# Attention heads finished at every second unit: the head two back is transposed, then scores, then its values; compressed values as split rows in one fp32r matmul each

## The chip, the cores and the metric

The kernel runs as one program on one core of a Trainium2 chip. The metric is the device time of one execution, in microseconds (us). Three runs of the kernel before took 2580.71, 2580.88 and 2580.91 us; the median is 2580.88.

A core has a matrix engine (PE), which reads its stationary operand by a weight load (PEld) and streams the moving one; a vector engine (DVE); a scalar engine (ACT); GpSimd (POOL); and SP, whose queue issues the weight DMAs here. Each engine runs its own instructions in their written order and waits for the others by semaphores.

## The reference, cut to what matters

The program is a stack of layers on x (1, 256, 2048) in fp32: a Mamba2 mixer, a conv FFN, a sparse attention mixer (NSA), a second conv FFN. The change touches the attention alone. There are 16 heads in 4 key groups (KVG = 4, HPG = 4 heads in each), 128 values per head, 256 positions (two chunks of L = 128). With 256 positions each query sees compressed keys (15 of them), all earlier selected blocks, and the window:

```python
q = rms_norm(q.reshape(bsz, seq, G, HG, DH), q_norm)
p_c = masked_softmax(einsum('btghd,bngd->bghtn', qb, k_cmp) * scale, cmp_end <= t)
o_c = einsum('bghtn,bngd->btghd', p_c, v_cmp)          # 15 compressed keys
p_s = masked_softmax(...);  o_s = einsum(p_s, vg)      # selected blocks
p_w = masked_softmax(...);  o_w = einsum(p_w, vwb)     # window
o = gb[0] * o_c + gb[1] * o_s + gb[2] * o_w
return o @ w_out
```

## The kernel before, in words

**Every projection is streamed in units.** A unit is 8 blocks of 128x128 fp32 weights (512 KB). SP loads it into one of RING = 4 slots of `raw` (L386 on); ACT rounds it to `w_hi` (fp32r, L441); DVE forms `w_lo` = `raw` - `w_hi` (L1268); PE multiplies 8 blocks with two fp32r matmuls each, one of `w_lo` on 256 columns (L843) and one of `w_hi` on 512 (L844). ACT may round unit v + 4 only when PE has used unit v, because both share a slot:

```python
if not isinstance(w, int) or w >= RING:
    act.wait_ge(unit_used, w - RING + 1)
```

DVE's split of unit v + 4 then waits for that rounding. Two units make a tile of 128 outputs. When a tile is complete (after an odd unit), ACT copies one half of its sums (`take_cross`, L450) and DVE adds and scales it (`tile_sum`, L1273 and L1277).

**The query phase** (`q`) has four bodies of 8 units, v = 0 to 7, and each body gives the queries of the four heads of one group. Body g computes the queries of group g, while the attention of group G = g - 1 is woven between its units. The order on each engine is written out by hand in `attend`, `before` and `q_body`: what stands there for unit v is issued after PE's unit v, and on ACT and DVE before or after the round or the split of unit v + 4. Body 0 has no attention, body 1 is that of G = 0, and a loop runs bodies 2 and 3 (G = 1 and 2). Group 3 comes in `last_heads`, among the first four units of the output projection `nsa_out`.

**One head** goes through these steps, each in a function of one engine:
- `scores` (PE, L1124 to L1127): four fp32 matmuls of 143, 271, 128 and 256 columns.
- `mask` and `shift` (DVE, L1608 to L1627): mask, row maxima, and the shift `nm` for the exponentials. For a group's first head, `shift` first takes the reciprocal `rq` of the query norms (L1625), which PE has turned into columns (`turn_query_roots`, L1114).
- `exps` (ACT, L724): six exponentials with sums.
- `normalise` (DVE, L1635 to L1647): reciprocal of the sums, gates, and the scaling of the probabilities. It raises `probs_ready`.
- `turn_probs` (PE, L1137 and L1139): seven transposes of the probabilities into `pq`.
- `pt0_copy` (ACT, L730, L731) and `pt1_copy` (DVE, L1652): PSUM to SBUF.
- `outputs` (PE, L1151 and L1154): six fp32 matmuls of 128 columns on the values, two more on the 15 compressed values.
- `o_round` (ACT, L735) and `o_rest` (DVE, L1658): the head's output as high and low parts.

In the kernel before, PE does `scores(h)` and `outputs(h - 2)` after even unit 2h and `turn_probs(h - 1)` after the odd unit behind it. `query_sums` and `query_roots` form the norms of a group's queries once for each group.

Of the kernel before, what the change touches and what calls it, by code (L numbers as in the profile page):

```python
# [54 lines left out]
ROWS = 32  # L55

# [87 lines left out]
def trunk(nc, x_in, consts_in, head_in, w_ssm_in, w_ssm_out, w_gu0, w_gu1, w_down0, w_down1, w_nsa_in,  # L144
# [19 lines left out]
    with ctx:  # L164
# [58 lines left out]
        with ExitStack() as st:  # L223
# [12 lines left out]
            vcn = sb("vcn", [ROWS + NCMP, KVG, P], F32, st)  # L236
            vcs = sb("vcs", [ROWS + NCMP, P], F32, st)
# [22 lines left out]
            pts = [kv[:, 8:12].rearrange("p (b a) t -> p b (a t)", b=2), q[:, 9:13].rearrange("p (b a) t -> p b (a t)", b=2)]  # L260
            v_st = kv[:, 6:8].rearrange("p a t -> p (a t)")
# [66 lines left out]
        vcmp_moved, vcn_zero = sem("vcmp_moved"), sem("vcn_zero")  # L328
        kdiag_ready, kbc_done = sem("kdiag_ready"), sem("kbc_done")
# [98 lines left out]
        def _(act):  # L428
# [299 lines left out]
            def pt0_copy(G, h):  # L728
                act.wait_ge(turned_p, G * HPG + (h + 1))
                act.activation(pts[h % 2][:, 0, 0:3 * L], ps[6][:, 0:3 * L], ACT.Copy)  # L730
                act.activation(pts[h % 2][0:ROWS + NCMP, 0, 3 * L:4 * L], ps[6][0:ROWS + NCMP, 3 * L:4 * L], ACT.Copy).then_inc(pt0_ready, 1)  # L731

# [5 lines left out]
            def query_roots(G):  # L738

                act.wait_ge(qss_done, G + 1)  # L740
                act.wait_ge(qstd_turned, G)
                act.activation(psq[:], ps[6][:, 0:T], ACT.Sqrt, bias=eps[:, 1:2]).then_inc(qstd_ready, 1)

            def before(G, v):

                if v == 1:
                    o_round(G, 2)
                    pt0_copy(G, 3)
                if v == 3:
                    o_round(G, 3)  # L750

            def attend(G, v):

                if v == 0:
                    query_roots(G)
                if v >= 5 and v % 2:
                    o_round(G, v // 2 - 2)
                if v >= 3 and v % 2:
                    pt0_copy(G, v // 2 - 1)
                if v % 2:  # L760
                    exps(G, v // 2)

            def q_body(g):
                p = ph["q"]
                for v in range(p.body):
                    round_unit(p.unit0 + RING + v, UNIT, g, p.body)
                    if v % 2:
                        take_cross(p, g, v // 2)
                    if not is_body(g, 0):
                        if not is_body(g, 1):  # L770
                            before(g - 2, v)
                        attend(g - 1, v)
# [19 lines left out]
            def last_heads(G):  # L792

                o_round(G - 1, 2)
                query_roots(G)
# [26 lines left out]
        def _(pe):  # L822
# [276 lines left out]
            def query_sums(G):  # L1099

                pe.wait_ge(qsq_ready, HPG * (G + 1))
                if not is_body(G, 0):
                    pe.wait_ge(pt0_ready, HPG * G - 1)
                for h in range(HPG):
                    mm = pe.matmul(ps[6][h * ROWS:(h + 1) * ROWS, 0:T], ones[:, 0:ROWS], qsq[:, h], start=True, stop=True)
# [24 lines left out]
            def turn_probs(G, h):  # L1130
# [4 lines left out]
                for b in range(2):  # L1135
                    for a in range(3):
                        mm = pe.transpose(ps[6 + b][:, a * L:(a + 1) * L], prs[u][:, b, a * L:(a + 1) * L], ident[:])  # L1137
                    if b == 0:
                        pe.transpose(ps[6][0:ROWS + NCMP, 3 * L:4 * L], prc[:, u].rearrange("p c n -> p (c n)")[:, 0:ROWS + NCMP], ident[:])  # L1139
                mm.then_inc(turned_p, 1)  # L1140

            def outputs(G, h):
# [14 lines left out]
            def before(G, v):  # L1157

                if v == 0:
                    outputs(G, 2)  # L1160
                if v == 1:
                    pe.wait_ge(qstd_ready, G + 2)
                    turn_probs(G, 3)
                if v == 3:
# [12 lines left out]

            def q_body(g):
                if is_body(g, 1):
                    pe.wait_ge(k_ready, 5)  # L1180
                for v in range(ph["q"].body):
                    gemm_unit(ph["q"], g, v, xn)
                    if not is_body(g, 0):
                        if v == 1:
                            turn_query_roots(g - 1)
                        if is_body(g, 1):
                            attend(g - 1, v)
                        elif v == 0:
                            attend(g - 1, v)
                            before(g - 2, v)  # L1190
                        else:
                            before(g - 2, v)
                            attend(g - 1, v)
# [25 lines left out]
            def last_heads(G):  # L1219

                scores(G, 0)
# [37 lines left out]
        def _(dve):  # L1259
# [370 lines left out]
            def normalise(G, h):  # L1630
# [29 lines left out]
            def before(G, v):  # L1660

                if v == 0:
                    normalise(G, 3)
                if v == 1:
                    o_rest(G, 2)
                    pt1_copy(G, 3)
                if v == 3:
                    o_rest(G, 3)
# [280 lines left out]
```

## Time and profile before

| what | value |
|---|---|
| median of 3 runs | 2580.88 us |
| the profiled execution | 2582.43 us |
| its span in the profile | 2580.7 us |
| PE busy | 2571.8 us (100%) |
| DVE busy | 1791.1 us (69%) |
| ACT busy | 1424.0 us (55%) |
| POOL busy | 223.2 us (9%) |

The profiled execution took 1.73 us more than its span. The table is read from the top: PE is busy through all of the span, and the others have slack on the average. The query phase with attention lies at about 1598 to 1765 us of the span.

### The profile page before, as it was taken

Reading aid. Unit: us, or ns where it says so; the run is one execution under the profiler, and the core shown is the slowest. Engines: PE = TensorE matmul, PEld = TensorE weight load, DVE = VectorE, ACT = ScalarE, POOL = GpSimd, SP = SyncE. Lnnn points to the kernel's source line nnn. Section 1 sums busy time; section 2 is a strip of 40 time slices with the busy share of each in tenths; the row PEclk is TensorE's granted clock in tenths of the full one; section 3 lists DMA queues with packets and bytes.
Section 4 is the critical chain, followed back from the end, with each engine's and each line's share of the span. In section 5 each row is a group of like instructions: output and inputs, shape, how many; then the busy total and the mean of one; then the engine's idle time right before and its main releaser. Section 6 shows DMA issues by size and latency. Waiting matters only on the chain.

```text
span 2580.7 us, 46167 instructions
## 1 busy us (share of the span) xinstructions
PE 2571.8 (100%) x15247; PEld 2257.7 (87%) x15247; DVE 1791.1 (69%) x2590; ACT 1424.0 (55%) x2206; POOL 223.2 (9%) x199
## 2 busy tenths in 40 slices
PE   9999999999999999999999999999999999999999
PEld 8888888888888888888888888888888888888888
DVE  8777777765677777776555686777777777775444
ACT  6776766754455555554444455666555555554443
POOL 0211122222100000000111000102200000000000
PEclk9999999999999999999999999999999999999999
DMA  6665555656555556556666676334555556556665
GB/s 212 230 196 195 190 197 194 199 172 189 187 191 189 187 189 191 190 188 187 188 189 193 193 233 200 124 98 134 184 191 188 188 190 191 191 186 186 189 191 167
DMA packets 139483, 481.59 MB, mean 187 GB/s; under 512 B 17329, under 2 KB 19441, under 8 KB 138384
## 3 DMA queue, kind: packets, MB, share of 16 engines
q1 hardware_dynamic: 136448, 467.20, 57.8%
q0 software_dynamic: 2368, 12.68, 1.4%
q8 instruction: 47, 0.77, 0.1%
q10 hardware_dynamic: 592, 0.71, 0.1%
q14 instruction: 28, 0.23, 0.0%
HBM read 478.28 MB, written 2.16 MB: 186 GB/s over the span
## 4 chain that ended last, share of the span: by engine, by line
PE 95%; DVE 3%; ACT 1%; issue 1%; DMA 0%; POOL 0%; ACTq 0%; DVEq 0%
PE ps L844 49%; PE ps L843 26%; PE pq L844 6%; PE po L844 3%; PE pq L843 3%; PE po L843 2%; DVE w_lo L1268 1%; PE po L1151 1%; PE pq L1137 0%; PE ps L975 0%; ACT w_hi L441 0%; PE ps L958 0%; PE pq L861 0%; PE ps L977 0%; PE pq L862 0%
## 5 line engine op out<-in xcount | busy, mean ns | idle before, releaser
L1268 DVE TENSOR_TENSOR w_lo<-raw,w_hi 128x1024 fp32r<-128x1024 f32 (+1 forms) x896 | 1094.2, 1224 | 627.2 <-ACT w_hi L441 625.8
L441 ACT ACTIVATE w_hi<-raw 128x1024 fp32r<-128x1024 f32 (+1 forms) x896 | 933.7, 1044 | 808.6 <-PE ps L844 701.8
L844 PE MATMUL ps<-xn,w_hi 128*128 128x512 f32 x3904 | 1358.9, 392 | 0.0
L843 PE MATMUL ps<-xn,w_lo 128*128 128x256 f32 x3904 | 1099.6, 282 | 0.3 <-DVE gpad L1277 0.2
L844 PEld LDWEIGHTS ps<-xn,w_hi 128*128 128x128 f32 x3904 | 731.6, 187 | 158.2
L843 PEld LDWEIGHTS ps<-xn,w_lo 128*128 128x128 f32 x3904 | 738.8, 189 | 4.1 <-issue 1.7
L844 PE MATMUL ps<-hid,w_hi 128*128 128x512 f32 x1408 | 488.2, 392 | 0.0
L843 PE MATMUL ps<-hid,w_lo 128*128 128x256 f32 x1408 | 394.7, 280 | 0.0
L844 PEld LDWEIGHTS ps<-hid,w_hi 128*128 128x128 f32 x1408 | 263.7, 187 | 57.4
L843 PEld LDWEIGHTS ps<-hid,w_lo 128*128 128x128 f32 x1408 | 266.5, 189 | 0.0
L844 PE MATMUL pq<-xn,w_hi 128*128 128x512 f32 x528 | 185.4, 393 | 0.0
L843 PE MATMUL pq<-xn,w_lo 128*128 128x256 f32 x528 | 152.7, 289 | 0.1
L643 ACT ACTIVATE hid<-up 128x256 f32 (+1 forms) x88 | 36.8, 418 | 180.4 <-DVE up L1523 180.4
L844 PEld LDWEIGHTS pq<-xn,w_hi 128*128 128x128 f32 x528 | 99.1, 188 | 23.4 <-issue 1.7
L450 ACT ACTIVATE cross<-ps 128x256 f32<-128x256 f32 x296 | 107.7, 364 | 9.0 <-PE ps L844 9.0
L844 PE MATMUL po<-xn,w_hi 128*128 128x512 f32 x304 | 107.2, 394 | 0.0
L843 PEld LDWEIGHTS pq<-xn,w_lo 128*128 128x128 f32 x528 | 99.9, 189 | 2.4 <-issue 1.4
L1514 DVE SCALAR_TENSOR_TENSOR gcv<-gpad,cst,gcv 128x256 f32<-128x256 f32 x176 | 84.9, 482 | 13.2 <-DVE gcv L1514 13.1
L844 PE MATMUL ps<-o_nsa,w_hi 128*128 128x512 f32 x256 | 89.3, 393 | 0.0
L844 PE MATMUL pq<-y_ssm,w_hi 128*128 128x512 f32 x256 | 89.1, 392 | 0.0
L843 PE MATMUL po<-xn,w_lo 128*128 128x256 f32 x304 | 85.9, 283 | 0.0
L1526 DVE TENSOR_TENSOR hid<-up,hid 128x256 f32 (+1 forms) x88 | 37.4, 425 | 63.5 <-ACT hid L643 63.5
(296 smaller groups left out, 2466.8 us busy)
## 6 DMA issues: line engine op xcount, KB each, us to landing
raw<-w_gu SPq DMA_DIRECT2D x352, 512.0 KB, 3.9
raw<-w_ssm_in SPq DMA_DIRECT2D x158, 512.0 KB, 3.9
raw<-w_down SPq DMA_DIRECT2D x128, 448.0 KB, 3.5
raw<-w_nsa_in SPq DMA_DIRECT2D x82, 512.0 KB, 4.1
raw<-w_ssm_out SPq DMA_DIRECT2D x64, 512.0 KB, 4.3
raw<-w_down SPq DMA_DIRECT2D x64, 512.0 KB, 3.7
raw<-w_nsa_out SPq DMA_DIRECT2D x32, 512.0 KB, 4.3
wcum<-cum_scratch POOLq DMA_DIRECT2D x8, 1024.0 KB, 7.8
```

What stands on the lines that cost most here:

```text
L441: act.activation(w_hi[:, slot, 0:n * P], raw[:, slot, 0:n * P], ACT.Copy).then_inc(unit_rounded, 1)
L450: act.activation(cross[:, (p.tile0 + k) % 2, 0:n], bank(p, i, k)[:, n:2 * n], ACT.Copy).then_inc(cross_copied, 1)
L643: act.activation(hid[:, bass.ds(j, 1), 0:T], up[:].rearrange("p (o t) -> p o t", o=1), ACT.Copy).then_inc(hid_rounded, 1)
L843: pe.matmul(acc[:, n:2 * n], w_lo[:, slot, cols], x[:, kb, 0:n], start=(kb == 0), stop=False, skip_group_check=True)
L844: mm = pe.matmul(acc[:, 0:2 * n], w_hi[:, slot, cols], x[:, kb, 0:2 * n], start=False, stop=(kb == n_blocks - 1), skip_group_check=True)
L1151: pe.matmul(o[:, c], v_st[:, (2 * b + a) * P:(2 * b + a + 1) * P], pth[:, b, cut], start=(a + b == 0), stop=False)
L1268: TT(w_lo[:, slot, 0:n * P], raw[:, slot, 0:n * P], w_hi[:, slot, 0:n * P].bitcast(F32), ALU.subtract).then_inc(unit_split, 1)
L1514: STT(gcv[:], gpad[:, a:a + T], cst[:, bass.ds(j * 3 + (CONST["ffn_conv_w"] + 3 * l * FFN_TILES + a), 1)], gcv[:], ALU.mult, ALU.add).then ...
L1526: TT(row[:, T:2 * T], up[:], row[:, 0:T].bitcast(F32), ALU.subtract).then_inc(hid_ready, 1)
```

## The change

On all three engines the odd places of a body are emptied of the transposes and what follows them, and everything of a finished head comes at one even place:
- PE, after even unit 2h: `turn_probs(h - 2)`, `scores(h)`, `outputs(h - 2)`; at v = 0 also `query_sums` behind them. After odd units nothing, but for `turn_query_roots` at v = 1. Heads are counted through the groups: at v = 0 and 2 the head two back is head 2 or 3 of the group before.
- ACT: `pt0_copy(h - 2)` before the round at even places; `o_round(h - 2)` and `exps(h)` after the cross copy at odd ones.
- DVE: `pt1_copy(h - 2)`, `mask(h)`, `shift(h)` at even places; `normalise(h - 1)` and `o_rest(h - 2)` behind split and tile sum at odd ones. `shift(0)` moves from v = 0 to v = 1, and the last head of the group before is normalised at v = 0.
- `last_heads`: `turn_probs(2, 2)`, `pt0_copy` and `pt1_copy` of that head now stand at its start, since the last odd place no longer holds them; on ACT `query_roots` goes ahead of `o_round(2, 2)`.

The compressed values are split into high and low parts. `vcs` holds for each chunk 45 rows (high, high, low: three times 15) at rows 0 and 64, and the probabilities, scaled, stand as (high, low, high) in `prq` next to each other, so that one fp32r matmul of 45 rows takes the place of an fp32 matmul of 15 rows. `normalise` writes the high part twice (one instruction) and the low part by two more; `pt0_copy` writes the turned rows to `pcz` in fp32r. At the start the values are split once more and moved by five DMAs in place of one. `query_sums` goes to bank `ps[4]`.

```diff
             def outputs(G, h):
...
                 for c in range(2):
-                    at = slice(c * ROWS, c * ROWS + NCMP)
-                    mm = pe.matmul(o[:, c], vcs[at], pth[at, 0, 3 * L:4 * L], start=False, stop=True)
+                    at = slice(c * HALF, c * HALF + STACK)
+                    mm = pe.matmul(o[:, c], vcs[at], pcz[at, h % 2], start=False, stop=True)
                 mm.then_inc(o_done, 1)
 
+            def attend(G, v):
+
+                h = v // 2
                 if v == 1:
-                    pe.wait_ge(qstd_ready, G + 2)
-                    turn_probs(G, 3)
-                if v == 3:
-                    outputs(G, 3)
-
-            def attend(G, v):
-
-                if v % 2 == 0:
-                    scores(G, v // 2)
+                    turn_query_roots(G)
+                if v % 2:
+                    return
+                earlier = (G, h - 2) if h >= 2 else None if is_body(G, 0) else (G - 1, h + 2)
+                if earlier:
+                    turn_probs(*earlier)
+                scores(G, h)
+                if earlier:
+                    outputs(*earlier)
                 if v == 0:
                     query_sums(G)
-                if v >= 3 and v % 2:
-                    turn_probs(G, v // 2 - 1)
-                if v >= 4 and v % 2 == 0:
-                    outputs(G, v // 2 - 2)
...
             def last_heads(G):
 
+                turn_probs(G - 1, 2)
                 scores(G, 0)
...
             def normalise(G, h):
...
-                TT(prc[:, u, :, 0:NCMP], prc[:, u, :, 0:NCMP], cf[:, h, 0:2].unsqueeze(2).broadcast_to([P, 2, NCMP]), ALU.mult)
+                parts = prq[u][:, :, 0:STACK].rearrange("p c (t n) -> p c t n", t=3)
+                TT(parts[:, :, 0:3:2].bitcast(F32R), prc[:, u, :, 0:NCMP].unsqueeze(2).broadcast_to([P, 2, 2, NCMP]),
+                   cf[:, h, 0:2].unsqueeze(2).unsqueeze(3).broadcast_to([P, 2, 2, NCMP]), ALU.mult).then_inc(cmp_hi, 1)
                 for c, cut in enumerate((slice(0, L), slice(L, 3 * L))):
                     rows = prs[u][:, :, cut]
+                    if c:
+                        dve.wait_ge(cmp_hi, H + 1)
+                        for d in range(2):
+                            STT(parts[:, d, 1], prc[:, u, d, 0:NCMP], cf[:, h, d:d + 1], parts[:, d, 0], ALU.mult, ALU.subtract)
                     last = TT(rows, rows, by_c[:, 1:3, c:c + 1].broadcast_to([P, 2, (c + 1) * L]), ALU.mult)
...
             def attend(G, v):
# DVE
-                if v >= 2 and v % 2 == 0:
-                    normalise(G, v // 2 - 1)
+                h = v // 2
+                earlier = (G, h - 2) if h >= 2 else None if is_body(G, 0) else (G - 1, h + 2)
                 if v % 2 == 0:
-                    mask(G, v // 2)
-                    shift(G, v // 2)
-                if v >= 5 and v % 2:
-                    o_rest(G, v // 2 - 2)
-                if v >= 3 and v % 2:
-                    pt1_copy(G, v // 2 - 1)
+                    if earlier:
+                        pt1_copy(*earlier)
+                    mask(G, h)
+                    if h:
+                        shift(G, h)
+                    elif earlier:
+                        normalise(G - 1, 3)
+                else:
+                    if h:
+                        normalise(G, h - 1)
+                    else:
+                        shift(G, 0)
+                    if earlier:
+                        o_rest(*earlier)
```

**On DVE**, in the looped body, from one odd place to the next even one. Before, behind the two splits (units 2 and 3 of the ring ahead) and the tile sum (L1273, L1277):

```order
L1268 TENSOR_TENSOR w_lo<-raw,w_hi 128x1024
L1273 TENSOR_TENSOR q<-ps,cross 128x256
L1277 TENSOR_TENSOR q<-q,rstd 128x256
L1658 TENSOR_TENSOR o_nsa<-po,o_nsa 128x256
L1652 COPY kv<-pq 128x384
L1635 TENSOR_SCALAR den<-den 128x6
L1637 RECIPROCAL den<-den 128x6
L1639 TENSOR_TENSOR cf<-den,gate_t 128x6
L1644 TENSOR_TENSOR prc<-prc,cf 128x2x15
L1647 TENSOR_TENSOR pr<-pr,cf 128x2x128
L1647 TENSOR_TENSOR pr<-pr,cf 128x2x256
L1608 TENSOR_TENSOR prc<-ps,mskc 128x2x15
```

Here `normalise` is that of the head whose exponentials ACT forms at this very odd place. After the change the same stretch reads (the line numbers are those of the changed file: L1257 is the split, L1262 and L1266 the tile sum, L1653 `o_rest`, L1647 `pt1_copy`):

```order
L1257 TENSOR_TENSOR w_lo<-raw,w_hi 128x1024
L1262 TENSOR_TENSOR q<-ps,cross 128x256
L1266 TENSOR_TENSOR q<-q,rstd 128x256
L1624 TENSOR_SCALAR den<-den 128x6
L1626 RECIPROCAL den<-den 128x6
L1628 TENSOR_TENSOR cf<-den,gate_t 128x6
L1634 TENSOR_TENSOR kv<-prc,cf 128x2x2x15
L1642 TENSOR_TENSOR pr<-pr,cf 128x2x128
L1641 SCALAR_TENSOR_TENSOR kv<-prc,cf,kv 128x15 x2
L1642 TENSOR_TENSOR pr<-pr,cf 128x2x256
L1653 TENSOR_TENSOR o_nsa<-po,o_nsa 128x256
L1647 COPY kv<-pq 128x384
```

`normalise` still stands behind the odd split and tile sum, but now it is that of the head before, and the copy of the turned probabilities comes behind it.

**On PE**, in the looped body, from the end of an odd unit to the start of the next odd one. Before (matmuls of the unit between the two places left out, one pair shown):

```order
L1137 MATMUL pq<-ident,pr 128x128 x3
L1139 MATMUL pq<-ident,prc 47x128
L1137 MATMUL pq<-ident,pr 128x128 x3
L843 MATMUL ps<-xn,w_lo 128x256
L844 MATMUL ps<-xn,w_hi 128x512
L1124 MATMUL ps<-kc,q 128x143
L1125 MATMUL ps<-kc,q 128x271
L1126 MATMUL ps<-kv,q 128x128
L1127 MATMUL ps<-kv,q 128x256
L1151 MATMUL po<-q,kv 128x128 x6
L1154 MATMUL po<-q,vcs 128x128 x2
```

After the change (L845 and L846 are the unit's pair, L1139 and L1141 the transposes, L1126 to L1129 the scores, L1153 and L1156 the outputs):

```order
L845 MATMUL ps<-xn,w_lo 128x256
L846 MATMUL ps<-xn,w_hi 128x512
L1139 MATMUL pq<-ident,pr 128x128 x3
L1141 MATMUL pq<-ident,q 109x128
L1139 MATMUL pq<-ident,pr 128x128 x3
L1126 MATMUL ps<-kc,q 128x143
L1127 MATMUL ps<-kc,q 128x271
L1128 MATMUL ps<-kv,q 128x128
L1129 MATMUL ps<-kv,q 128x256
L1153 MATMUL po<-q,kv 128x128 x6
L1156 MATMUL po<-pcz,vcs 128x128 x2
```

The seven transposes have moved from behind the odd unit to behind the even one that follows it, ahead of the scores, and the outputs of the same head follow in the same place.

**On ACT**, at the change from v = 1 to v = 2 of the looped body. Before (L441 round, L450 cross copy, L735 `o_round`, L730 and L731 `pt0_copy`, L724 `exps`, six in all of which the first and the last stand):

```order
L441 ACTIVATE w_hi<-raw 128x1024
L450 ACTIVATE cross<-ps 128x256
L735 ACTIVATE o_nsa<-po 128x256
L730 ACTIVATE q<-pq 128x384
L731 ACTIVATE q<-pq 47x128
L724 ACT_TABLE_LOAD
L724 ACTIVATE prc,den<-prc,nm,rq 128x15
L724 ACTIVATE pr,den<-pr,nm,rq 128x256
L441 ACTIVATE w_hi<-raw 128x1024
```

After the change (L447 round, L456 cross copy, L741 `o_round`, L730 `exps`, L736 and L737 `pt0_copy`):

```order
L447 ACTIVATE w_hi<-raw 128x1024
L456 ACTIVATE cross<-ps 128x256
L741 ACTIVATE o_nsa<-po 128x256
L730 ACT_TABLE_LOAD
L730 ACTIVATE prc,den<-prc,nm,rq 128x15
L730 ACTIVATE pr,den<-pr,nm,rq 128x256
L736 ACTIVATE q<-pq 128x384
L737 ACTIVATE pcz<-pq 109x128
L447 ACTIVATE w_hi<-raw 128x1024
```

The two copies of the turned probabilities stood ahead of the exponentials of the group's first head; now they stand behind them.

## Rows read from the trace of the kernel before

**Rows 1.** The page: busy time of each engine, the chain by engine.
```profile
PE 2571.8 (100%) x15247; PEld 2257.7 (87%) x15247; DVE 1791.1 (69%) x2590; ACT 1424.0 (55%) x2206; POOL 223.2 (9%) x199
PE 95%; DVE 3%; ACT 1%; issue 1%; DMA 0%; POOL 0%; ACTq 0%; DVEq 0%
```
**Rows 2.** Timeline of PE at an odd place: start us, duration us, what.
```profile
1679.90 0.40 PE L844 MATMUL ps<-xn,w_hi 128*128 128x512 f32 x1
...
1680.25 0.40 PE L844 MATMUL ps<-xn,w_hi 128*128 128x512 f32 x1
1680.49 0.49 PE L1137 MATMUL pq<-ident,pr 128*128 128x128 f32 x3
...
1681.37 0.39 PE L844 MATMUL ps<-xn,w_hi 128*128 128x512 f32 x1
```
**Rows 3.** Timeline of ACT behind the same place.
```profile
1680.68 1.06 ACT L441 ACTIVATE w_hi<-raw 128x1024 fp32r<-128x1024 f32 x1 [4.43 <-PE ps L844]
...
1682.18 0.49 ACT L730 ACTIVATE q<-pq 128x384 f32<-128x384 f32 x1
...
1682.70 0.40 ACT L724 ACTIVATE prc<-prc,nm,rq 128x15 f32<-128x15 f32 x1
...
1685.59 1.06 ACT L441 ACTIVATE w_hi<-raw 128x1024 fp32r<-128x1024 f32 x1
```
**Rows 4.** Timeline of DVE behind the same place.
```profile
1681.78 1.23 DVE L1268 TENSOR_TENSOR w_lo<-raw,w_hi 128x1024 fp32r<-128x1024 f32 x1 [1.91 <-ACT w_hi L441]
...
1683.71 0.42 DVE L1658 TENSOR_TENSOR o_nsa<-po,o_nsa 128x256 f32 x1
...
1685.73 0.17 DVE L1635 TENSOR_SCALAR den<-den 128x6 f32<-128x6 f32 x1 [1.14 <-ACT pr L724]
...
1686.57 1.02 DVE L1647 TENSOR_TENSOR pr<-pr,cf 128x256 f32<-128x256 f32 x2
...
1688.93 0.17 DVE L1627 SCALAR_TENSOR_TENSOR nm<-mx,rq 128x6 f32<-128x6 f32 x1
1689.03 1.23 DVE L1268 TENSOR_TENSOR w_lo<-raw,w_hi 128x1024 fp32r<-128x1024 f32 x1
```
**Rows 5.** The chain of waits at the first head: start us, us, what.
```profile
1629.72 1.03 DVE pr L1647 x2
1630.75 0.04 issue
1630.80 0.55 PE pq L1137 x3
```
**Rows 6.** Groups of PE by form, 1600 to 1775 us: busy us, mean ns.
```profile
L1137 PE MATMUL pq<-ident,pr 128*128 128x128 f32 x90 | 14.2, 276 | 0.2 <-DVE pr L1647 0.2
L1137 PE MATMUL pq<-ident,q 128*128 128x128 f32 x6 | 1.0, 277 | 0.7 <-DVE kv L1652 0.7
```
**Rows 7.** Timelines of PE and DVE at v = 1 of G = 2.
```profile
1700.46 0.40 PE L844 MATMUL ps<-xn,w_hi 128*128 128x512 f32 x1
...
1701.05 0.53 PE L1137 MATMUL pq<-ident,pr 128*128 128x128 f32 x3
...
1701.33 0.21 DVE L1625 RECIPROCAL rq<-ps 128x8 f32<-128x8 f32 x1 [2.71 <-PE ps L1114]
1701.57 0.17 DVE L1627 SCALAR_TENSOR_TENSOR nm<-mx,rq 128x6 f32<-128x6 f32 x1
```
**Rows 8.** The chain of waits in `last_heads`.
```profile
1737.29 1.28 ACT L742
...
1751.67 0.42 PE po L1154 x4
```
**Rows 9.** Timeline of PE: scores between two units.
```profile
1626.04 0.39 PE L844 MATMUL ps<-xn,w_hi 128*128 128x512 f32 x1
...
1627.74 0.39 PE L844 MATMUL ps<-xn,w_hi 128*128 128x512 f32 x1
```
**Rows 10.** Stretches: PE, PEld, DVE, ACT, POOL busy, granted clock, DMA share, GB/s.
```profile
1602.00:1765.00 163.00, 161.94 (x1071) 140.60 (x1070) 117.99 (x377) 110.29 (x303) 16.73 (x24) 1.00 0.33 107
```

More of the change, by code:

```diff
@@ L55 @@
 ROWS = 32
+HALF = 64
+STACK = 3 * NCMP
 F32 = mybir.dt.float32
@@ L260, in trunk @@
             pts = [kv[:, 8:12].rearrange("p (b a) t -> p b (a t)", b=2), q[:, 9:13].rearrange("p (b a) t -> p b (a t)", b=2)]
+            prq = [pts[u % 2][:, u // 2, 3 * L:4 * L].rearrange("p (c n) -> p c n", c=2) for u in range(3)]
+            vcl = o_nsa[0:NCMP, D_TILES - 1]
             v_st = kv[:, 6:8].rearrange("p a t -> p (a t)")
@@ L741, in query_roots @@
                 act.wait_ge(qstd_turned, G)
[L742 to L748, printed above, removed]
-                if v == 3:
-                    o_round(G, 3)
-            def attend(G, v):
-                if v == 0:
-                    query_roots(G)
-                if v >= 5 and v % 2:
-                    o_round(G, v // 2 - 2)
-                if v >= 3 and v % 2:
-                    pt0_copy(G, v // 2 - 1)
+                act.activation(psq[:], ps[4][:, T:2 * T], ACT.Sqrt, bias=eps[:, 1:2]).then_inc(qstd_ready, 1)
+            def attend(G, v):
+                h = v // 2
+                earlier = (G, h - 2) if h >= 2 else None if is_body(G, 0) else (G - 1, h + 2)
+                if v % 2 == 0 and earlier:
+                    pt0_copy(*earlier)
                 if v % 2:
-                    exps(G, v // 2)
+                    if earlier:
+                        o_round(*earlier)
+                    exps(G, h)
             def q_body(g):
@@ L765, in q_body @@
                 for v in range(p.body):
+                    if not is_body(g, 0) and v % 2 == 0:
+                        attend(g - 1, v)
                     round_unit(p.unit0 + RING + v, UNIT, g, p.body)
@@ L769, in q_body @@
                     if not is_body(g, 0):
-                        if not is_body(g, 1):
-                            before(g - 2, v)
-                        attend(g - 1, v)
+                        if v == 0:
+                            query_roots(g - 1)
+                        if v % 2:
+                            attend(g - 1, v)
                     elif v == 0:
@@ L792, in last_heads @@
             def last_heads(G):
+                pt0_copy(G - 1, 2)
+                query_roots(G)
                 o_round(G - 1, 2)
-                query_roots(G)
                 exps(G, 0)
@@ L1101, in query_sums @@
                 pe.wait_ge(qsq_ready, HPG * (G + 1))
-                if not is_body(G, 0):
-                    pe.wait_ge(pt0_ready, HPG * G - 1)
+                if is_body(G, 0):
+                    pe.wait_ge(vt_ready, KVG)
                 for h in range(HPG):
-                    mm = pe.matmul(ps[6][h * ROWS:(h + 1) * ROWS, 0:T], ones[:, 0:ROWS], qsq[:, h], start=True, stop=True)
+                    mm = pe.matmul(ps[4][h * ROWS:(h + 1) * ROWS, T:2 * T], ones[:, 0:ROWS], qsq[:, h], start=True, stop=True)
                 mm.then_inc(qss_done, 1)
@@ L1183, in q_body @@
                     if not is_body(g, 0):
[L1184 to L1193, printed above, removed]
+                        attend(g - 1, v)
                     elif v == 0:
@@ L1658, in o_rest @@
                 TT(lo, out_banks(G, h), hi.bitcast(F32), ALU.subtract).then_inc(o_ready, 1)
[L1660 to L1668, printed above, removed]
             def attend(G, v):
-                if v >= 2 and v % 2 == 0:
-                    normalise(G, v // 2 - 1)
+                h = v // 2
+                earlier = (G, h - 2) if h >= 2 else None if is_body(G, 0) else (G - 1, h + 2)
                 if v % 2 == 0:
-                    mask(G, v // 2)
-                    shift(G, v // 2)
-                if v >= 5 and v % 2:
-                    o_rest(G, v // 2 - 2)
-                if v >= 3 and v % 2:
-                    pt1_copy(G, v // 2 - 1)
+                    if earlier:
[10 more added lines that the diff above has]
+                        shift(G, 0)
+                    if earlier:
+                        o_rest(*earlier)
             def q_body(g):
@@ L1722, in q_body @@
                         dve.memset(prc[:], FLOOR).then_inc(floor_set, 1)
-                        dve.wait_ge(floor_set, 1)
+                        for u in range(3):
+                            dve.memset(prq[u], 0.0).then_inc(floor_set, 1)
+                        dve.wait_ge(floor_set, 4)
             def late_split(u):
```

30 lines of the change are left out of this document (16 added, 14 removed).

## The prediction

> **What bounds the kernel now.** I read the page first, then the waits of PE, then the timelines of all three engines through one head. The page says that PE is busy for 2571.8 of 2580.7 us and that 95% of the chain is PE's [rows 1]: time is what PE issues, plus what PE is made to wait. In the attention phase PE stands still almost nowhere: the transposes, the one step of PE that needs a chain through ACT and DVE, wait 0.2 us at the first head and 0.7 us in `last_heads`, and no other group there has idle time to speak of [rows 6]. The averages (DVE 69%, ACT 55%) say that there is slack, but not where. What matters here is how long after PE's odd unit the two other engines can have a head's probabilities ready. That is read from the timelines.
>
> Take the end of an odd unit as time s. In the rows it is 1680.49, where the transposes follow the last L844 [rows 2]. ACT may round the unit four ahead only when this unit has been used: it had been idle for 4.43 us and starts at 1680.68, s + 0.19 [rows 3]. DVE, idle for 1.91 us until that rounding, starts its split at 1681.78, s + 1.29; split and tile sum are over at 1683.71, **s + 3.22** [rows 4]. Neither engine was late from work of its own, so this offset is set by PE's own unit and moves with it. The reader should see that whatever stands behind the odd split on DVE can't begin before s + 3.22, however long its operands have been ready.
>
> **The change part by part.**
>
> *Transposes one unit behind the odd place.* `normalise(h - 1)` now stands directly behind the odd tile sum, and PE wants its result after the next even unit. One unit is 8 pairs at 0.35 us (1679.90 to 1680.25, [rows 2]), 2.8 us. So PE is there at s + 2.8. DVE begins `normalise` at s + 3.22. It takes 1.86 us (1685.73 to 1686.57 + 1.02, [rows 4]). The change adds two small instructions on 15 elements; the nearest row is the shift's, 0.10 us from its start to the next one's (1688.93 to 1689.03, [rows 4]), so 0.20; the doubled write of the high part I put at 0.05, an estimate. Ready at 3.22 + 1.86 + 0.25 = s + 5.33; PE takes it up 0.05 later, as between 1630.75 and 1630.80 [rows 5]: s + 5.38. **PE waits 2.6 us.** Before, the same `normalise` stood ahead of the even split and was bound by the exponentials (idle 1.14 us until ACT, [rows 4]), with a whole unit in hand: done at s + 7.1 (1687.59), while PE needed it only behind transposes, a unit, scores, outputs and one more unit. That the exponentials are now done long before is of no use: they are no longer what is late.
>
> How often: heads 0, 1 and 2 of each group are normalised at an odd place (v = 3, 5, 7) and transposed one unit later (v = 4, 6, and 0 of the next body). For G = 0 and 1 that is six, for G = 2 two (heads 0 and 1): 8 x 2.6 = **20.8 us**. Head 3 is normalised at v = 0 and transposed at v = 2, behind two units: no wait. Queued behind the waiting transposes on PE are the scores, outputs and all later units; ACT and DVE wait for those in turn, so the next s moves along and the wait comes again in full.
>
> *Head 2 of group 2.* It is normalised at v = 7 of the last body, and `last_heads` begins with its transposes, with no unit in between: PE waits from s to s + 5.38, **5.4 us**.
>
> *ACT at the change of group.* `pt0_copy(G - 1, 3)` now stands behind `exps(G, 0)`, and these wait for `shift(G, 0)`, which has moved behind the odd tile sum. From s of unit 1: shift from 3.22, reciprocal to the next start 0.24 and the shift itself 0.17 (1701.33, 1701.57, [rows 7]), 3.63; exponentials 2.89 (1682.70 to 1685.59, [rows 3]), 6.5; the copies 0.52 (1682.18 to 1682.70, [rows 3]), 7.05, and 0.1 for the two hand-overs. PE wants to start the outputs after the turn of the roots 0.36 (1701.05 less the unit's end at 1700.69, [rows 7]), a unit 2.8, transposes 0.77 (1680.25 to 1681.37 less a pair, [rows 2]) and scores 1.35 (1626.04 to 1627.74 less a pair, [rows 9]): s + 5.28. It waits 1.85 us, for G = 1 and 2: **3.7 us**. The table load of 1.28 us is started by ACT while it waits, and costs nothing here. At the other places the copies follow the transposes that PE itself was late with, on an ACT whose exponentials end before that (at s + 5.1 even with the copies ahead of them, [rows 3]), and they take less than half of the time of the scores: hidden; uncovered they would be 0.5 us for each head. For G = 0 no head is turned at v = 2, but the scores of head 1 wait for the reciprocal at s + 3.46, with PE there at 3.16: **0.3 us**.
>
> *What PE issues.* Transposes, scores and the six matmuls on the values are as many as before; only where they stand differs, and an odd place that falls away gives next to nothing back, since seven transposes at an insertion cost 0.77 us for their own work. The two matmuls on the compressed values of a head took 0.42 us in fp32 [rows 8]. No row has an fp32r matmul of 128 columns. The nearest is the unit's pair, 768 columns in 0.35 us, so 0.117 for 256. I take 0.117 for each of the two (nothing in the rows shows that half the columns take half the time), 0.23 for a head; gain 0.19 x 16 = **3.0 us**. At one end each costs half of it (0.06), gain 4.8 us; at the other it costs what the fp32 one did, gain 0.
>
> The Trainium skill ("TensorE: Matmul & The Clock Gate", section on LDWEIGHTS) gives a load time by columns, whatever the rows, which is 107 ns for 128 columns. By that the two together take at least 0.21 us and the gain is 3.3 us, an estimate from the page; the lower end of 0.06 would be out.
>
> *The rest.* The first head's wait of 0.2 us is contained in the new ones: -0.2. In `last_heads` ACT now loads the root's table before it waits, so 1.28 us leave the chain [rows 8]; but the roots then wait for PE's sums anyway, `o_round` comes behind them, and each `normalise` of the chain that ends in the 0.7 us wait is 0.25 longer. I take nothing, with -1.0 and +0.5 as ends. The clearing of `prq`, the second split of the values and four DMAs more fall in body 0, a full body before the first outputs, beside DVE and POOL that wait for PE: nothing; if that cover were gone, some 2 us.
>
> The sum: 20.8 + 5.4 + 3.7 + 0.3 - 3.0 - 0.2 = **27.0 us**. The profiled execution's span of 2580.7 becomes 2607.7, and with the 1.7 us around it 2609.4 in that execution's own time of 2582.43 before. The median of before is 2580.88, 1.55 below that execution, so I forecast 2607.9, rounded **2608**.
>
> **The rivals.**
>
> *The clock falls in the long wait.* The clock is granted in full (1.00, 2.4 GHz) through the phase [rows 10], and the longest wait in the phase is 0.7 us [rows 6]. A wait of 5.4 us is new. If the clock then goes to its other level and stays there through the transposes, scores and unit behind it (0.77 + 1.35 + 2.8 = 4.9 us), these take 4.9 us more: 2612.8. For it: the length. Against: no row shows the lower level at all. The same page of the Trainium skill, in its part on the clock gate, says that an idle PE is throttled to half and gets its clock back only by sustained work; that is this rival, and no run so far shows it here.
>
> *The fp32r matmul of 128 columns is no cheaper.* Then the 3.0 us are gone: 2610.9. Nothing in the rows is against it, since the narrowest fp32r matmul has 256 columns.
>
> *The wait is real but shorter.* Were DVE's work behind s over by s + 4.0 in place of 5.4, the wait would be 1.2 us and the sum 8 x 1.2 + 4.0 + 3.7 + 0.1 = 17.4, less the gain of 3.0: 2595. For it: the rounding of 1.06 us would have to begin earlier than the used unit allows. The 4.43 us of ACT's idle time before it [rows 3] speak against that.
>
> *Faster after all.* If the probabilities were ready when PE comes, all waits go, the 0.2 us too, and only the gain is left: 2580.9 - 3.0 - 0.9 = 2577. The point from which it decides is one number: DVE must be done by s + 2.8. It would need `normalise` ahead of the odd split. That the head is now two back speaks for it on the face of it; rows 4 and the order on DVE speak against.
>
> **How the numbers follow.** The forecast as worked out: 0.62. Clock rival 0.15, no cheaper matmul 0.12 (both slower still), shorter wait 0.06, faster 0.04, and 0.01 for no change. Measurements of this kernel tell changes of about 0.2% (5 us) from none. So slower 0.95, same 0.01, faster 0.04. The likeliest case alone has 2605 to 2612 by the ends of the matmul's price, of the extra work in `normalise` (0.1 to 0.5 for nine heads) and of `last_heads`. The range takes in the two slower rivals and a little of the shorter wait: 2602 to 2615.
>
> **What would show it.** In the changed kernel's waits of PE, the transposes should stand first, waiting for DVE's `pr`: eight times about 2.6 us and once about 5.4. The first value matmul should wait for ACT's copy to `pcz` twice, about 1.9 us. On DVE, `normalise` should begin right behind the tile sum, 3.2 us after the odd unit's end, with no idle time for ACT ahead of it. The fp32r matmuls of 45 rows should follow each other at 0.12 us. The granted clock around the long wait tells the first rival. The prediction is wrong if the transposes don't wait, or if the waits are there and units run faster elsewhere to pay for them.

## The result, and the profile of the changed kernel

The changed kernel takes **2625.87 us** (median of 4 runs, 2624.49 to 2627.72) against 2580.89 us (median of 4 runs, 2580.71 to 2581.47) for the kernel before: a ratio of 1.0169, interval 1.0157 to 1.0181. It is 45 us slower. The forecast was 2608, the range 2602 to 2615: the sign was right, the size was not, and the time lies outside the range.

The page of the changed kernel answers to [rows 1]: busy time of each engine, and the granted clock in 40 slices of the span (9 is full).

```profile
PE 2584.1 (99%) x15215; PEld 2265.3 (86%) x15215; DVE 1798.7 (69%) x2626; ACT 1424.3 (54%) x2206; POOL 222.0 (8%) x203
...
PEclk9999999999999999999999999989999999999999
```

PE executes 32 instructions fewer than before (the two fp32 matmuls on the compressed values stood as four, the fp32r ones stand as two, for 16 heads) and is busy 12.3 us *longer*. That is the first sign that waits are not the whole story. The second is the slice of the clock that isn't 9: it lies in the attention phase. The profiled execution took 2624.49 us, its span is 2622.8.

The waits of PE from 1590 to 1800 us (for what, us in total, times, longest) answer to [rows 6]:

```profile
PE pq L1139 <- DVE pr L1642: 27.0, 9, 5.4
PE po L1153 <- issue: 3.6, 2, 1.8
PE pq L1139 <- DVE kv L1647: 1.0, 1, 1.0
PE ps L1126 <- issue: 0.2, 1, 0.2
```

These are the forecast waits: eight of 2.6 to 2.8 us and one of 5.4 for the transposes (forecast 26.2 in all), two of 1.8 for the outputs (3.7), one of 0.2 for the scores of head 1 (0.3). With the wait of 1.0 in `last_heads`, and less the 0.9 us of waits that the kernel before had, they explain 31 us. They don't explain 42, the difference of the spans (2622.8 less 2580.7).

What is left shows when two places with the same work are laid side by side. The timeline of PE (start us, duration, instruction, in brackets the idle time before it) at the first even place that waits, and at the second:

```profile
1635.91 0.55 PE L1139 MATMUL pq<-ident,pr 128*128 128x128 f32 x3 [2.79 <-DVE pr L1642]
...
1636.73 0.41 PE L1126 MATMUL ps<-kc,q 128*128 128x143 f32 x2
1636.98 0.62 PE L1127 MATMUL ps<-kc,q 128*128 128x271 f32 x2
...
1638.09 1.50 PE L1153 MATMUL po<-kv 128*128 128x128 f32 x12
1639.52 0.33 PE L1156 MATMUL po<-pcz,vcs 45*128 45x128 f32 x2
1639.78 0.39 PE L845 MATMUL ps<-xn,w_lo 128*128 128x256 f32 x1
...
1648.28 0.87 PE L1139 MATMUL pq<-ident,pr 128*128 128x128 f32 x3 [2.69 <-DVE pr L1642]
...
1649.80 0.69 PE L1126 MATMUL ps<-kc,q 128*128 128x143 f32 x2
1650.28 1.11 PE L1127 MATMUL ps<-kc,q 128*128 128x271 f32 x2
...
1652.12 1.50 PE L1153 MATMUL po<-q,kv 128*128 128x128 f32 x12
```

From the first transpose to the first output it is 2.18 us at the one place and 3.84 at the other. Transposes and scores of the second place take longer, while the outputs take 1.50 at both. The stretches of the same time (from:to, us, busy time of PE, PEld, DVE, ACT and POOL, granted clock, DMA share, GB/s) say why:

```profile
1600.00:1830.00 230.00, 198.15 (x1177) 171.34 (x1176) 143.15 (x436) 123.86 (x321) 24.24 (x37) 0.93 0.28 93
1645.00:1652.00 7.00, 4.32 (x19) 3.70 (x18) 3.99 (x13) 4.00 (x13) 0.61 (x1) 0.76 0.25 76
1652.00:1659.00 7.00, 7.00 (x46) 6.13 (x45) 3.61 (x13) 2.00 (x6) 0.00 (x0) 1.00 0.22 75
```

With the wait the granted clock fell, and at the outputs it was back. From the first of the scores to the second 0.48 us pass (1649.80 to 1650.28) in place of 0.25 (1636.73 to 1636.98): about the factor of two between the levels of 2.4 and 1.2 GHz. In this execution it fell so at seven of the eight short waits (all but the first) and at the long one. From the first transpose to the unit's first matmul, a short one costs 1.66 or 1.67 us more than the place without a fall at five of the seven, and 1.37 and 1.47 at the two of v = 0. The kernel before had 1.00 through the phase [rows 10].

The fall doesn't always come within the wait. At two places PE was already through the first three transposes: at the fourth (below) these take 0.55 as at full clock, and the outputs 1.65, so that they too are in part at the lower level. At the long wait the level was back before the unit, whose matmuls start again at their full rate:

```profile
1688.74 0.55 PE L1139 MATMUL pq<-ident,pr 128*128 128x128 f32 x3 [2.63 <-DVE pr L1642]
...
1692.44 1.65 PE L1153 MATMUL po<-kv 128*128 128x128 f32 x12
...
1774.59 0.63 PE L1129 MATMUL ps<-kv,q 128*128 128x256 f32 x2
...
1775.18 0.39 PE L846 MATMUL ps<-o_nsa,w_hi 128*128 128x512 f32 x1
```

On DVE, an odd place of the changed kernel whose unit ended on PE at about 1697.2 (the rows to set against [rows 4]):

```profile
1698.46 1.23 DVE L1257 TENSOR_TENSOR w_lo<-raw,w_hi 128x1024 fp32r<-128x1024 f32 x1 [2.67 <-ACT w_hi L447]
...
1700.40 0.16 DVE L1624 TENSOR_SCALAR den<-den 128x6 f32<-128x6 f32 x1
...
1701.37 0.42 DVE L1642 TENSOR_TENSOR pr<-pr,cf 128x256 f32<-128x256 f32 x1
1701.70 0.37 DVE L1641 SCALAR_TENSOR_TENSOR q<-prc,cf,q 128x15 f32<-128x15 f32 x2
1701.99 0.69 DVE L1642 TENSOR_TENSOR pr<-pr,cf 128x512 f32<-128x512 f32 x1
1702.60 0.42 DVE L1653 TENSOR_TENSOR o_nsa<-po,o_nsa 128x256 f32 x1
```

As forecast, `normalise` stands directly behind the tile sum without idle time, 3.2 us after the unit. It takes 2.28 us (1700.40 to 1702.68) where 2.11 were forecast (1.86 and 0.25) and 1.86 were needed before.

On ACT, the change of group (v = 1 of G = 1): the exponentials wait for the shift, the copies stand behind them.

```profile
1674.90 0.40 ACT L730 ACTIVATE prc<-prc,nm,rq 128x15 f32<-128x15 f32 x1 [0.56 <-DVE nm L1616]
...
1677.80 0.47 ACT L736 ACTIVATE q<-pq 128x384 f32<-128x384 f32 x1
1678.17 0.26 ACT L737 ACTIVATE pcz<-pq 109x128 fp32r<-109x128 f32 x1
```

PE starts the outputs at 1678.53, 0.1 after the second copy ends, having stood still for 1.77 us. The waits call this releaser "issue", and only the timelines side by side show that it is the copy.

### The profile page after: what moved, and what is told of

It is laid out like the page before. It is cut to its first block and busy times, and to the rows that moved or that the text cites. A ratio compares the mean times of both kernels' runs of the same rounds, so it can differ in the third digit from the quotient of the medians.

```text
span 2622.8 us, 46145 instructions
## 1 busy us (share of the span) xinstructions
PE 2584.1 (99%) x15215; PEld 2265.3 (86%) x15215; DVE 1798.7 (69%) x2626; ACT 1424.3 (54%) x2206; POOL 222.0 (8%) x203
## 5 line engine op out<-in xcount | busy, mean ns | idle before, releaser
L1257 DVE TENSOR_TENSOR w_lo<-raw,w_hi 128x1024 fp32r<-128x1024 f32 (+1 forms) x896 | 1093.5, 1222 | 651.0 <-ACT w_hi L447 649.6
L447 ACT ACTIVATE w_hi<-raw 128x1024 fp32r<-128x1024 f32 (+1 forms) x896 | 933.5, 1044 | 819.0 <-PE ps L846 713.3
L846 PE MATMUL ps<-xn,w_hi 128*128 128x512 f32 x3904 | 1358.6, 392 | 0.0
L845 PE MATMUL ps<-xn,w_lo 128*128 128x256 f32 x3904 | 1097.6, 281 | 0.4 <-DVE gpad L1266 0.2
L846 PEld LDWEIGHTS ps<-xn,w_hi 128*128 128x128 f32 x3904 | 730.4, 187 | 159.6
L845 PEld LDWEIGHTS ps<-xn,w_lo 128*128 128x128 f32 x3904 | 737.7, 189 | 5.0 <-issue 2.3
L846 PE MATMUL ps<-hid,w_hi 128*128 128x512 f32 x1408 | 488.2, 391 | 0.0
L845 PE MATMUL ps<-hid,w_lo 128*128 128x256 f32 x1408 | 394.2, 280 | 0.0
L846 PEld LDWEIGHTS ps<-hid,w_hi 128*128 128x128 f32 x1408 | 263.3, 187 | 57.7
L845 PEld LDWEIGHTS ps<-hid,w_lo 128*128 128x128 f32 x1408 | 266.1, 189 | 0.0
L846 PE MATMUL pq<-xn,w_hi 128*128 128x512 f32 x528 | 185.1, 392 | 0.0
L845 PE MATMUL pq<-xn,w_lo 128*128 128x256 f32 x528 | 152.4, 289 | 0.1
L846 PEld LDWEIGHTS pq<-xn,w_hi 128*128 128x128 f32 x528 | 98.9, 187 | 23.3 <-issue 1.7
L456 ACT ACTIVATE cross<-ps 128x256 f32<-128x256 f32 x296 | 108.1, 365 | 9.0 <-PE ps L846 9.0
L846 PE MATMUL po<-xn,w_hi 128*128 128x512 f32 x304 | 107.2, 394 | 0.0
L845 PEld LDWEIGHTS pq<-xn,w_lo 128*128 128x128 f32 x528 | 99.8, 189 | 2.4 <-issue 1.7
L846 PE MATMUL ps<-o_nsa,w_hi 128*128 128x512 f32 x256 | 89.3, 392 | 0.0
L846 PE MATMUL pq<-y_ssm,w_hi 128*128 128x512 f32 x256 | 89.2, 392 | 0.0
L845 PE MATMUL po<-xn,w_lo 128*128 128x256 f32 x304 | 85.8, 282 | 0.0
```

The source lines that it names most:

```text
L447: act.activation(w_hi[:, slot, 0:n * P], raw[:, slot, 0:n * P], ACT.Copy).then_inc(unit_rounded, 1)
L456: act.activation(cross[:, (p.tile0 + k) % 2, 0:n], bank(p, i, k)[:, n:2 * n], ACT.Copy).then_inc(cross_copied, 1)
L845: pe.matmul(acc[:, n:2 * n], w_lo[:, slot, cols], x[:, kb, 0:n], start=(kb == 0), stop=False, skip_group_check=True)
L846: mm = pe.matmul(acc[:, 0:2 * n], w_hi[:, slot, cols], x[:, kb, 0:2 * n], start=False, stop=(kb == n_blocks - 1), skip_group_check=True)
L1257: TT(w_lo[:, slot, 0:n * P], raw[:, slot, 0:n * P], w_hi[:, slot, 0:n * P].bitcast(F32), ALU.subtract).then_inc(unit_split, 1)
```

## The experiments

Each ratio is against the kernel before, run beside it on the same chip. Its median there was 2581.72 us for four of the kernels (the one with `fill(12)`, the order alone, the values alone, `normalise` at the even place) and 2581.61 for the other four.

**Is it the clock?** The wait stays as long, but PE isn't idle in it: dummy matmuls into a bank that nobody reads stand ahead of the transposes.

```diff
+            def fill(n):
+                for _ in range(n):
+                    pe.matmul(ps[7][:, 3 * L:4 * L], ones[:], ident[:], start=True, stop=True)
...
                 if earlier:
+                    if h != 1:
+                        fill(12)
                     turn_probs(*earlier)
...
             def last_heads(G):
+                fill(25)
                 turn_probs(G - 1, 2)
```

> The changed kernel, with matmuls of 128 columns that nobody reads put on PE ahead of the transposes that wait: 12 (2.6 us) at each of the eight, 25 (5.3 us) at the one in last_heads. PE is kept busy through the waits, which stay as long as they are. Theory (some 14 to 16 us of the 45 are PE's work at the lower clock behind each wait): the granted clock is 1.00 in all stretches and the time falls from 2626 to about 2611 us. Rival (the idle time is all that counts, and the rest of the loss lies elsewhere): no change by more than 3 us.

Measured: 2611.43 us (2611.24 to 2611.92), ratio 1.0115 (1.0098 to 1.0132), so 14.4 us less than the changed kernel although PE has *more* to do (15.3 if each is set against the kernel before that was run beside it: 29.7 in place of 45.0). Timeline of PE at the second place that waits (an fp32 matmul stands as two instructions, so the 12 are x24):

```profile
1645.95 2.84 PE L1134 MATMUL pq<-ident,ones 128*128 128x128 f32 x24
1648.79 0.55 PE L1143 MATMUL pq<-ident,pr 128*128 128x128 f32 x3
...
1650.97 1.50 PE L1157 MATMUL po<-q,kv 128*128 128x128 f32 x12
```

The transposes start as late as before, but 2.18 us later PE is at the outputs, as at the one place of the changed kernel where the clock didn't fall. Over the whole phase:

```profile
1600.00:1830.00 230.00, 224.88 (x1493) 199.12 (x1492) 151.85 (x447) 130.64 (x331) 28.84 (x41) 1.00 0.32 103
```

Shown: the lower clock behind the waits is a cost of its own, 14 us, besides the idle time.

**How long may PE stand still?** Half the filling, `fill(6)` in place of `fill(12)`:

> The changed kernel with the filling matmuls of the eight short waits halved: 6 (1.3 us), then some 1.3 us idle; the long wait stays filled. Theory (the clock falls behind an idle stretch of 2.6 us but not behind 1.3): granted clock 1.00 and 2611 us, as with the full filling. Rival (any idle stretch at these places costs clock in proportion): about 2618 us.

Measured: 2611.39 us (2611.34 to 2611.75), ratio 1.0115 (1.0100 to 1.0131). The same time; PE stands still for 1.24 to 1.49 us at each of the eight places:

```profile
1645.30 1.50 PE L1134 MATMUL pq<-ident,ones 128*128 128x128 f32 x12
1648.10 0.55 PE L1143 MATMUL pq<-ident,pr 128*128 128x128 f32 x3 [1.30 <-DVE pr L1649]
...
1650.28 1.50 PE L1157 MATMUL po<-q,kv 128*128 128x128 f32 x12
```

Idle times of 1.24 to 1.49 us leave the clock at its upper level (1.00 over the phase).

**Is the wait set by what stands ahead of `normalise` on DVE?** It goes ahead of the tile sum:

```diff
             def attend(G, v):                  # DVE
                 else:
-                    if h:
-                        normalise(G, h - 1)
-                    else:
+                    if not h:
                         shift(G, 0)
...
                     split_unit(p.unit0 + RING + v, UNIT, g, p.body)
+                    if v % 2 and v > 1 and not is_body(g, 0):
+                        normalise(g - 1, v // 2 - 1)
                     if v % 2:
```

> The changed kernel with normalise(h - 1) between the odd split and the tile sum on DVE, 0.8 us earlier. Theory (the waits are s + X less one unit, and the clock falls only behind waits that are long enough): eight waits of 1.85 us and one of 4.6, 19.4 us in place of 27.0: 2618 us if the clock falls behind each as before, 2606 us if a wait of 1.85 us leaves it alone. The rival that DVE's place within an odd unit doesn't matter, since PE waits for something else: no change, 2626 us.

Measured: 2605.97 us (2604.71 to 2606.70), ratio 1.0092 (1.0077 to 1.0108). Six waits are 1.63 to 1.69 us, two (at v = 0) 1.88 and 1.92, the last 4.49. This kernel happens to show where the clock gives way. PE at the first place, and at the two places of v = 0 (G = 1 and 2):

```profile
1635.16 0.55 PE L1139 MATMUL pq<-ident,pr 128*128 128x128 f32 x3 [1.69 <-DVE pr L1642]
...
1658.13 0.52 PE L1139 MATMUL pq<-ident,pr 128*128 128x128 f32 x3 [1.88 <-DVE pr L1642]
...
1659.04 0.69 PE L1126 MATMUL ps<-kc,q 128*128 x2
...
1706.80 0.52 PE L1139 MATMUL pq<-ident,pr 128*128 128x128 f32 x3 [1.92 <-DVE pr L1642]
...
1707.59 0.41 PE L1126 MATMUL ps<-kc,q 128*128 x2
```

Scores that take 0.41 at full clock take 0.69 behind the wait of 1.88, and 0.41 behind that of 1.92, with the same work around both. So the length of the wait alone doesn't decide at about 1.9 us. All waits of 1.63 to 1.69 us left the clock full, the one of 4.49 didn't. The gain of 20 us is both costs together: about 9 us of idle time (27.0 became 18.3) and most of the clock's.

**Order and values apart.** First the new order with the old fp32 values: all edits to `vcn`, `vcs`, `pcz` and `prq` undone.

> The changed kernel's order with the old fp32 matmuls of 15 rows. Theory: normalise is 0.25 us shorter, so nine waits are 2.2 us shorter in sum, and the outputs are 2.6 us longer in sum: 2626 us, within 2 us of the changed kernel. Rival (the values cause part of the loss, by wider copies or a mode of the array): 2620 us or less.

Measured: 2624.63 us (2623.90 to 2625.61), ratio 1.0165 (1.0148 to 1.0182). The order alone loses 42.9 us of the 45.0. The waits of PE for the transposes:

```profile
PE pq L1138 <- DVE pr L1635: 23.9, 9, 5.1
```

They are 3.1 us less than the 27.0 of the full change, 0.34 at each of nine, since `normalise` is shorter without the split of the probabilities: 1.98 us in place of 2.28 at the place shown above. The clock fell at all nine, eight waits of 2.25 to 2.56 us and one of 5.07.

Then the kernel before with the split values alone (all edits to the compressed values, of which the one in `outputs` is shown):

```diff
-                    at = slice(c * ROWS, c * ROWS + NCMP)
-                    mm = pe.matmul(o[:, c], vcs[at], pth[at, 0, 3 * L:4 * L], start=False, stop=True)
+                    at = slice(c * HALF, c * HALF + STACK)
+                    mm = pe.matmul(o[:, c], vcs[at], pcz[at, h % 2], start=False, stop=True)
```

> The kernel before with the compressed values as split rows in one fp32r matmul, order untouched. Theory (0.26 us for the two matmuls of a head in place of 0.42): 16 x 0.16 = 2.6 us less, 2578.3 us, less what last_heads takes back. Rival (the two small instructions in normalise and the wider copies eat it): 2580 to 2582 us.

Measured: 2581.21 us (2580.99 to 2582.06), ratio 0.9999 (0.9989 to 1.0008): no change. A place with scores and outputs became 0.16 us shorter (3.15 in place of 3.31 over a pair), 2.6 us for 16 heads. The waits of PE grew from 0.9 to 2.7:

```profile
PE po L1157 <- DVE kv L1664: 1.1, 2, 0.5
PE pq L1143 <- DVE kv L1664: 1.0, 1, 1.0
PE pq L1143 <- DVE pr L1659: 0.6, 1, 0.6
```

The first row is new. At v = 3 of a body `pt1_copy` stood last on DVE and was done 0.34 us ahead of the outputs (1675.37 and 1675.71 in the kernel before, G = 1). From the start of the first head's `normalise` to the end of that copy DVE works without a pause, for 8.49 us in place of 7.88; 0.32 of the difference is `normalise` itself. Now the outputs of two heads wait half a microsecond each.

**Can that be mended?** The copy directly behind the odd split, ahead of the tile sum, is the version that the runs so far point to:

```diff
-                if v >= 3 and v % 2:
-                    pt1_copy(G, v // 2 - 1)
...
                     split_unit(p.unit0 + RING + v, UNIT, g, p.body)
+                    if v >= 3 and v % 2 and not is_body(g, 0):
+                        pt1_copy(g - 1, v // 2 - 1)
```

> The values alone, in the order before, with pt1_copy of v = 3, 5 and 7 directly behind the odd split on DVE, ahead of the tile sum and of o_rest. Theory (in the values alone, 1.1 us of the gain go into two waits of the outputs for this copy, which normalise has pushed back): the two waits of 0.54 us go, 2581.2 - 1.1 = 2580.1 us, about 1.5 us under the kernel before. Rival (the longer normalise then waits elsewhere): 2581 us as without it.

Measured: 2580.97 us (median of 11 runs, 2580.32 to 2581.46), ratio 0.9996 (0.9987 to 1.0005). The lowest median of the runs, 0.9 us above what I expected, and not told apart from the kernel before. The two waits only passed to the next in line, `o_rest`, which now stands behind the copy:

```profile
PE pq L1143 <- DVE kv L1664: 1.1, 1, 1.1
PE po L1157 <- DVE o_nsa L1670: 0.9, 2, 0.4
PE pq L1143 <- DVE pr L1659: 0.6, 1, 0.6
```

**The new order without its wait.** `normalise(h - 1)` goes behind the shift at even places, so it is done before the next odd unit ends:

```diff
             def attend(G, v):                  # DVE
                         shift(G, h)
+                        normalise(G, h - 1)
                 else:
-                    if h:
-                        normalise(G, h - 1)
-                    else:
+                    if not h:
                         shift(G, 0)
```

> One thing differs from the changed kernel: normalise(h - 1) on DVE stands at the even place behind shift(h), ahead of the even split, and no longer behind the odd tile sum. Theory (nine waits of PE for the probabilities, and the lower clock that each leaves behind, are all that the change lost): the nine waits go from 27.0 us to 0, the granted clock is 1.00, and what is left is two waits of 1.8 us for ACT's copies against 2.6 us gained on the compressed values: about 2582 us. Rival (doing transposes, scores and outputs in one place costs PE or the other engines something of its own): the waits go, but the time stays above 2588.

Measured: 2587.21 us (2586.62 to 2587.86), ratio 1.0022 (1.0012 to 1.0032). The waits for `pr` are gone and 39 us come back, but the 2582 that I expected missed by 5. The waits of PE now begin with

```profile
PE po L1153 <- issue: 5.5, 10, 1.8
```

3.6 us of which are the two at the change of group, as before. The other eight, 0.2 to 0.3 us each, are new. ACT at one of them:

```profile
1644.47 0.47 ACT L736 ACTIVATE q<-pq 128x384 f32<-128x384 f32 x1
1644.84 0.26 ACT L737 ACTIVATE pcz<-pq 109x128 fp32r<-109x128 f32 x1
```

and PE:

```profile
1645.20 1.58 PE L1153 MATMUL po<-q,kv 128*128 128x128 f32 x12 [0.32 <-issue]
```

ACT is at the read-out of the last exponential from 1644.38, and the copies follow and run to 1645.10, though the transposes began at 1642.60. With PE no longer late, ACT is still at the exponentials of the odd place when the transposes are done. The cover of the copies that the prediction named existed only because PE waited. The eight make 1.9 of the 5 us as idle time, and 3.2 with the 0.16 us that each wait costs beyond it (see the sum below); the rest was not tracked down.

**Both waits away.** In addition the head at the change of group is transposed at v = 1, as in the kernel before, and no longer at v = 2:

```diff
                 if v == 1:                     # PE
                     turn_query_roots(G)
+                    if not is_body(G, 0):
+                        turn_probs(G - 1, 3)
...
+                    if v == 1 and earlier:     # ACT
+                        pt0_copy(G - 1, 3)
                     exps(G, h)
...
+                        if not h:              # DVE, behind o_rest
+                            pt1_copy(G - 1, 3)
```

> On top of normalise at the even place: head 3 of the group before is turned at v = 1, as in the kernel before, so that its copy on ACT stands ahead of the exponentials of the new group's head 0. Theory: the two waits of 1.8 us go, and the outputs' waits of 0.2 to 0.3 us for copies (ten of them) stay: 2587.2 - 3.6 = 2583.6 us, still above the kernel before. Rival (the late copies come from something that only moves on): 2586 us or more.

Measured: 2582.91 us (2582.08 to 2585.35), ratio 1.0004 (0.9994 to 1.0013). The two waits of 1.8 us are gone:

```profile
PE po L1155 <- issue: 2.0, 8, 0.3
```

With the waits at the transposes and the two at the outputs undone, the changed kernel isn't told apart from the kernel before: the 2.6 us of the values pay for the small waits. The new grouping by itself is still a small loss. The kernel with the same values in the old order and the copy first, run beside this one, took 2580.97 us, 1.9 less, and the runs of the two don't overlap (2580.32 to 2581.46 against 2582.08 to 2585.35).

## Why the prediction was right in its waits and wrong in its sum

*The waits of the transposes: right.* Forecast 20.8 + 5.4, measured 27.0, by the mechanism given: DVE began `normalise` at s + 3.2, and one unit is too little. `normalise` took 0.17 more than I put, 1.5 over nine waits. Only 0.12 of its 0.42 over before is the new place, the rest the split: with the old values it takes 1.98 there. That the sum is only 0.8 over the forecast comes from how idle time is counted (below): by starts of matmuls, as I had forecast, the nine are about 28.4.

*The outputs at the change of group, and the scores of head 1: right.* 3.6 us for 3.7, and 0.2 for 0.3.

*The fp32r matmuls: nearly right, and lost elsewhere.* I chose 0.117 us each; the pair takes 0.26 (1639.52 to 1639.78), 0.13 each, a gain of 2.6 for 3.0. Beside it I should have priced the longer `normalise` once more: in the kernel before `pt1_copy` at v = 3 of a body had only 0.34 us to spare, and in the new order all that the split adds to `normalise` lies in a wait. In either order the gain came to nothing: values alone 0.5 us less than before, with an interval of the ratio that holds 1; in the new order 2625.87 with them and 2624.63 without.

*`last_heads`: about nothing, as taken.* The wait there is 1.0 us in place of 0.7.

*The clock: the step that failed.* The prediction put it into a rival with a chance of 0.15, for the long wait alone, and priced that fall at 4.9 us: 2612.8. Both halves were wrong. The short waits of 2.6 us, which it treated as idle time only, lower the clock as well, in seven of eight cases of the profiled execution. And the fall at the long wait costs 1.65 us, not 4.9, since the clock is back before the unit. The filled kernel gives the sum as a measurement, 14.4 us. The rule of the Trainium skill ("TensorE: Matmul & The Clock Gate", the part on the clock gate) that an idle PE is throttled was cited and is borne out by these rows; I had weighed it for one wait of nine. The evidence against it in the prediction, that no row shows the lower level, was no evidence: the longest idle time in the phase before was 0.7 us [rows 6], so no row there could have shown it.

The sum again, from the spans: transposes 27.0, outputs 3.6, scores 0.2, `last_heads` +0.3, values -2.6, the first wait -0.2, clock 12.6 (span 2622.8 less 2610.2 of the filled kernel): 40.9 of 42.1 us. The other 1.2 us lie in how the profile counts: idle time runs from the modelled end of the last matmul, but a matmul that needn't wait starts 0.16 us ahead of that end (1680.49 against 1680.25 + 0.40 in [rows 2]). For the eleven long waits that is 1.8 us, an estimate that is 0.6 too much. In the medians the clock's part is nearly 2 us larger than in the profiled execution (2624.49 was the fastest of the four), which fits its one place without a fall. The mean granted clock of the four runs points the same way (0.994 in the faster two, 0.993 in the slower two), but only that execution has a trace.

The expectation for `normalise` at the even place failed on the step "hidden" for ACT's copies. It was written for a PE that is late; once that lateness was taken away, the copies were next in line at eight places.

## What to carry to other kernels

A new wait on PE is not only its idle time. Here waits of about 2 us and more cost the work behind them at half the clock until the level returned: 1.4 to 1.7 us for a wait of 2.6, more than half as much again. "No row shows it" speaks against a mechanism only where the trace has a row in which it could have shown; and a cover by a wait ("hidden, since PE is late anyway") is gone as soon as someone mends the wait.

## What the runs showed of the hardware that I had not expected

- PE idle for 0.2 to 1.8 us kept the granted clock at its upper level in every case seen (eight waits of 1.24 to 1.49, six of 1.63 to 1.69, and those of 1.8 ahead of the outputs, two in each kernel that has them). Of two waits near 1.9 us one was followed by the lower level. All nine waits in the kernel with the order alone, of 2.25 us and more, were, and eight of nine in the changed kernel: the first, 2.79 us long, was not. What sets the exception is open. Behind each of the waits from 1.88 us on stand seven transposes; no run has other matmuls there, so whether they have a part in the fall is open too.
- A fall costs about the same at a wait of 5.4 us as at one of 2.6: from the last pair of a unit to the first of the next, less a pair's 0.35, the place took 9.38 us with it and 7.73 filled, a difference of 1.65, against 8.43 and 6.76 (1.67) at a short one.
- PE kept busy with dummy matmuls through a wait is 14 us faster over this phase than PE that waits: 2611.43 against 2625.87.
- Two fp32r matmuls of 45 rows and 128 columns take 0.26 us to the next start; two in fp32 on 15 rows took 0.42 [rows 8].
